# Half of the shift additions of two modulated norms move from VectorE to GpSimd

## The reference, cut to what matters

```python
def rmsnorm(x, w=None):
    y = xf * lax.rsqrt(jnp.mean(xf * xf, axis=-1, keepdims=True) + NORM_EPS)
    if w is not None: y = y * w
def modulate(h, shift, scale):
    return h * (1.0 + scale[:, None, :]) + shift[:, None, :]

h  = modulate(rmsnorm(x, norm1_w[l]), shift1, scale1);  proj = h @ w_in[l]
...
h2 = modulate(rmsnorm(x, norm2_w[l]), shift2, scale2);  ffn = hierarchical_moe(h2, ...)
```

## Time and profile before

| | |
|---|---|
| median of 3 runs | 3526.2 us (3526.06 to 3530.25) |
| profiled execution: time, span | 3523.97 us, 3522.1 us |
| granted TensorE clock over that span | 0.949 of full speed |
| busy: PE, DVE, ACT, POOL | 3103.1, 1535.7, 1125.4, 1110.3 us |

### The profile page before, as it was taken

The page is one execution under the profiler, slowest core; times in us unless marked ns, Lnnn a source line. Parts: engine busy times, 40 slices in busy tenths (PEclk is TensorE's granted clock), DMA queues, the critical chain, the costliest instruction groups (busy, mean ns, idle before and its releaser), DMA issues. The chain is left out here.

```text
span 3522.1 us, 40464 instructions
## 1 busy us (share of the span) xinstructions
PE 3103.1 (88%) x14608; PEld 2227.7 (63%) x14608; DVE 1535.7 (44%) x2012; ACT 1125.4 (32%) x1505; POOL 1110.3 (32%) x562
## 2 busy tenths in 40 slices
PE   6999999989999999769698997999594899999993
PEld 4666666468888788634343455999342677777772
DVE  4444444421111211336400334444415687878775
ACT  3333333011111122210210221222202677777773
POOL 1000110223333344400001213222000577878784
PEclk9999999999999999879799998999796899999996
DMA  2000001211111232145300004000303899999995
GB/s 86 24 25 19 25 25 59 91 47 52 50 48 48 77 119 93 57 185 179 146 24 23 30 31 174 13 13 1 124 9 123 286 372 371 368 368 375 365 375 214
DMA packets 116368, 450.06 MB, mean 128 GB/s; under 512 B 14609, under 2 KB 15569, under 8 KB 111265
## 3 DMA queue, kind: packets, MB, share of 16 engines
q1 hardware_dynamic: 103074, 396.83, 30.7%
q0 software_dynamic: 7856, 28.64, 2.4%
q10 hardware_dynamic: 5328, 23.07, 1.6%
HBM read 404.30 MB, written 44.10 MB: 127 GB/s over the span
## 5 line engine op out<-in xcount | busy, mean ns | idle before, releaser
L2685 DVE TENSOR_TENSOR moe_w_low<-moe_raw_up,moe_w_high 128x1024 fp32r<-128x1024 f32 x288 | 436.4, 1554 | 156.2 <-ACT moe_w_high L2625 156.2
L2548 POOL TENSOR_TENSOR moe_w_low<-moe_raw_down,moe_w_high 128x1024 fp32r<-128x1024 f32 x144 | 417.0, 2925 | 148.6 <-ACT moe_w_high L2635 148.6
L2625 ACT ACTIVATE moe_w_high<-moe_raw_up 128x1024 fp32r<-128x1024 f32 x288 | 304.9, 1062 | 187.5 <-PE ps L2588 110.3
L91 PE MATMUL ps<-x1T_high,w_up_high 128*128 128x512 f32 x704 | 274.7, 390 | 3.5 <-PEq L2906 3.5
L91 PE MATMUL ps<-x1T_low,w_up_high 128*128 128x512 f32 x704 | 274.3, 390 | 0.0
L91 PE MATMUL ps<-x1T_high,w_up_low 128*128 128x512 f32 x704 | 274.3, 390 | 0.0
L2603 PE MATMUL ps<-moe_w_high,moe_x_high 128*128 128x512 f32 x576 | 229.1, 398 | 4.2 <-DVE moe_x_low L2716 4.2
L2605 PE MATMUL ps<-moe_w_high,moe_x_low 128*128 128x512 f32 x576 | 226.0, 392 | 0.0
L2604 PE MATMUL ps<-moe_w_low,moe_x_high 128*128 128x512 f32 x576 | 225.6, 392 | 0.0
L764 POOL TENSOR_TENSOR w_up_high<-w_up,consts 128x1024 fp32r<-128x1024 f32 x44 | 83.5, 1897 | 382.7 <-PE ps L91 285.1
L272 POOL TENSOR_TENSOR qkv_low<-qkv_raw,qkv_high 128x1024 fp32r<-128x1024 f32 x22 | 53.6, 2436 | 468.3 <-ACT qkv_high L564 468.3
(11 more groups left out here) (433 smaller groups left out, 6147.4 us busy)
## 6 DMA issues: line engine op xcount, KB each, us to landing
moe_raw_up<-in_w SPq DMA_DIRECT2D x288, 512.0 KB, 10.2
moe_raw_down<-in_w SPq DMA_DIRECT2D x144, 512.0 KB, 9.1
w_ada<-in_w_ada SPq DMA_DIRECT2D x48, 512.0 KB, 4.6
w_up<-in_ffn_w_up SPq DMA_DIRECT2D x22, 1024.0 KB, 4.8
w_down<-in_ffn_w_down SPq DMA_DIRECT2D x44, 512.0 KB, 3.5
y_rows<-xT ACTq DMA_DIRECT2D x36, 512.0 KB, 8.2
qkv_raw<-in_attn_w SPq DMA_DIRECT2D x22, 512.0 KB, 3.5
y_rows<-zero_rows SPq DMA_DIRECT2D x1, 8192.0 KB, 29.1
```

The costliest lines, as they stand in the source:

```text
L91: ins = pe.matmul(out, stationary, moving, start=start and n == 0, stop=stop and n == last)
L2548: pool.tensor_tensor(w_low[:, down_slot(k)], raw_down[:, k], w_high[:, down_slot(k)].bitcast(F32), ALU.subtract).then_inc(down_low, 1)
L2625: act.activation(w_high[:, up_slot(n)], raw_up[:, n], ACT.Copy).then_inc(up_high, 1)
L2685: dve.tensor_tensor(w_low[:, up_slot(n)], raw_up[:, n], w_high[:, up_slot(n)].bitcast(F32), ALU.subtract).then_inc(up_low, 1)
```

## The change

In both norms the shift of the tiles with an even number (place 0 of `h`) is added by GpSimd, and that of the tiles with an odd number still by VectorE. The semaphore `shifted` becomes two, one for each place, and PE and SP wait for the one of their tile.

```diff
@@ in stage_modulated_norm
+        shifted = [sem(name + "_shifted0"), sem(name + "_shifted1")]
@@ dve
                 dve.scalar_tensor_tensor(h[:, s], m.res[:, t, :], inv[:, t:t + 1], scale, ALU.mult, ALU.mult
                                          ).then_inc(scaled, 1)
-                dve.wait_ge(scaled, t + 1)
-                dve.tensor_tensor(h[:, s], h[:, s], shift, ALU.add).then_inc(shifted, 1)
+                if s:
+                    dve.wait_ge(scaled, t + 1)
+                    dve.tensor_tensor(h[:, s], h[:, s], shift, ALU.add).then_inc(shifted[s], 1)
+
+        @block.gpsimd
+        def _(pool):
+            for t in range(0, TT, 2):
+                pool.wait_ge(scaled, t + 1)
+                pool.tensor_tensor(h[:, 0], h[:, 0], shift, ALU.add).then_inc(shifted[0], 1)
@@ pe
-                pe.wait_ge(shifted, t + 1)
+                pe.wait_ge(shifted[t % 2], t // 2 + 1)
@@ sp, norm2
-                    sp.wait_ge(shifted, t + 1)
+                    sp.wait_ge(shifted[t % 2], t // 2 + 1)
```

More of the change, by code:

```diff
@@ L1174, in stage_modulated_norm @@
         h = sb(name + "_h", [P, 2, D])
-        squared, meaned, rooted, inverted, scaled, shifted = (
-            sem(name + "_" + n) for n in ("squared", "meaned", "rooted", "inverted", "scaled", "shifted"))
+        squared, meaned, rooted, inverted, scaled = (
+            sem(name + "_" + n) for n in ("squared", "meaned", "rooted", "inverted", "scaled"))
+        shifted = [sem(name + "_shifted0"), sem(name + "_shifted1")]
         turned, turned_out = sem(name + "_turned"), sem(name + "_turned_out")
```

## The result

The changed kernel takes 3539.55 us in the median of 6 runs (3537.76 to 3543.28), the kernel before 3526.38 us (6 runs, 3525.41 to 3530.25). That is 13.2 us more, a ratio of 1.0037 with a 95% interval of 1.0024 to 1.0050. The forecast was 3537.1 us, +10.9 us, range 3532 to 3542. The profiled execution of the changed kernel took 3537.76 us against 3523.97, 13.8 us more, so one can look for the whole difference in the two traces.

A forecast was written before the change was run, and what follows sets the result against it. DVE alone was taken to set the pace in norm1, and norm2 to be held by its store as well; 5.5 us for norm1 and 5.4 for norm2 gave +10.9 on 3526.2, so 3537.1 us, range 3532 to 3542.

The forecast's parts named there:

- The turns at the port: Both norms: DVE instructions with two SBUF inputs and GpSimd's adds take turns whole, the waiting one going when the holder ends.
- the start of the first pair: Both norms: multiply 1 holds the port until 2.42 us, then GpSimd's add 0 goes and ends at 4.62.
- GpSimd's 2.34 us: Both norms: a shift on GpSimd costs 2.34 us instead of 1.22 us on the tile's own path.
- norm1: First norm: a pair of tiles cycles in 6.03 us, set by the port; +5.5 us with the last transposes' share.
- the last transposes: End of norm1: +0.9 us if PE has the slow clock there; half of it was taken.
- norm2: Second norm: place 0 comes back 2.73 us after GpSimd's end, so a pair cycles in 6.43 us; +5.4 us.
- The cycle is 1.28 + 0.08 + 2.34 + 2.73 = 6.43 us, above the 6.03 of the port: norm2, per pair: multiply, wake, GpSimd add and return of place 0 after its store set the pace, not the port.
- the same four pieces are then added in another order: norm1, if PE is fast: the odd multiply may go ahead of the GpSimd add, with the same pieces in the 6.03 us cycle.
- later ones 2.34: Sign in both norms: GpSimd's first add is 3.3 us long with its wait for the port, its later adds 2.34 us.
- No turns: Rival, both norms: DVE and GpSimd overlap freely; together +2.0 to +7.7 us, middle about 3531 us; chance 0.09.
- DVE keeps the port through its add: Rival, both norms: odd multiply and odd add both go ahead of the GpSimd add; about 3551 us; chance 0.05.
- Faster: Rival: DVE's freed 4.6 us in norm1 shows through unnoticed slack, norm2 gains nothing; 3521.6 us; chance 0.02.

The follow-up runs named there:

- PSUM experiment: The change, but VectorE reads the scale and shift rows from PSUM instead of SBUF; median 3531.23 us, 1.0015 of before.
- odd-multiply-waits experiment: The change, but VectorE waits ahead of each odd multiply until GpSimd has finished the even tile's shift; median 3535.55 us, 1.0031 of before.
- four places: The change, with four places for h instead of two and inputs still from SBUF; median 3531.68 us, 1.0015 of before.
- the two removals above: The change, with four places for h and VectorE's scale and shift rows in PSUM; median 3514.46 us, 0.9968 of before.

## Why the prediction was right, and where its size was off

- **Direction and mechanism.** Right. The turns at the port, the start of the first pair and GpSimd's 2.34 us were read from rows of other stages, and the traces show them here: GpSimd's first add was forecast to run from 1.36 to 4.62 and ran from 1.37 to 4.68. The PSUM experiment shows that it is VectorE's second SBUF input.
- **norm1.** Even multiplies forecast at 6.66, 12.69 and 18.72 us, measured 6.74, 12.71 and 18.67; last add 24.83, measured 24.71. For the last transposes half of 0.9 us was taken, and the slow 1.97 us came in full. The term was 5.5 and is 5.84 us.
- **norm2.** This term was mis-sized: 5.4 against 8.07 us. The step that failed is "The cycle is 1.28 + 0.08 + 2.34 + 2.73 = 6.43 us, above the 6.03 of the port". It takes the two limits as separate and the larger one as the pace. But they meet. The prediction asked only whether the store of tile 5 holds multiply 7, and not when tile 1's gives place 1 back. By its own terms add 1 ends at about 5.7 and place 1 is back 2.73 us later, at 8.4, while GpSimd wakes for tile 2 at 7.35 + 1.36 = 8.71: the odd multiply goes first. In the trace it starts at 8.74 and GpSimd asks at 8.85. Its 1.1 us then lie on the way round place 0, and since the two adds again end 1.08 us apart, the next pair meets in the same order. The cycle is 2.55 for the two multiplies, 2.20 for the add, 2.79 for the store: 7.54 us. The odd-multiply-waits experiment puts the cycle back to 6.48. Of the 2.7 us that the term lacks, 2.2 are the two cycles between multiplies 2 and 6; most of the rest is at the end, where tile 6's transposes now stand right ahead of tile 7's. Whether norm2 would keep the cheaper order by itself, once in it, no run shows. The sentence "the same four pieces are then added in another order" is nearly true where the port is the limit (5.68 us a pair with four places, 5.97 in norm1's order) and wrong where the ring is. The mark "later ones 2.34" failed in norm2 for the same reason.
- **The sum.** 10.9 was forecast; the profiles differ by 13.8 and the medians by 13.2 us. The interval of the medians' ratio, 8 to 18 us in time, holds both 10.9 and 13.9; only the stages show that the sum was too small. That the range held the result is partly luck: its width was meant for the last transposes, the hand-overs and the difference between runs, and it happened to cover a wrong cycle in norm2.
- **The rivals.** "No turns" was excluded by the stretched adds of 3.24 us, and where it was built its price was right for norm2 (27.99 us; the forecast for slow transposes was 24.01 + 3.7 = 27.7), and norm1's +0.9 us lies between its two prices of -0.3 and +4.0. "DVE keeps the port through its add" never happened: add 1 asked 1.15 us after GpSimd in norm1's first pair and went behind it, and so it was in norm2's pairs. "Faster" could not come by any slack; it took the two removals above.

## What to carry to other kernels

Before an elementwise operation moves to GpSimd, look at what VectorE does beside it: here it had two SBUF inputs, the two took turns, and the work was added instead of overlapped (5.68 us a pair with four places). With one of the inputs from PSUM (a constant row, copied while VectorE was idle), they overlapped fully (3.64 us). A slower engine in a ring also lengthens the way round a place; here the ring had to grow, too, before the move paid. And where two limits exist, the one can put its wait into the path of the other: ask in which order the engines arrive, pair by pair, and not only which limit is longer.

## What the runs showed of the hardware that was not expected

A bare wait made a stage faster: norm2 fell from 32.08 to 28.90 us when VectorE held back its odd multiply. Without that wait the odd multiply was first at the port by 0.1 us, and this cost 1.06 us a pair (7.54 against 6.48). A blocked instruction counts as busy: VectorE's adds show 3.24 us of which about 2.03 are waiting, and no idle time appears before them. Reading a 128x1024 float32 row from PSUM instead of SBUF changed the multiply only from 1.28 to 1.27 us.
